# A chunked scan in a three-block network: six places for the decay matrices, both directions added ahead of one product

## What is computed

```python
def step(h, inp):
    qq, kk, vv, aa = inp
    cs = jnp.cumsum(aa, axis=1)
    seg = cs[:, :, None] - cs[:, None, :]
    decay = jnp.exp(jnp.where(mask[None, :, :, None, None], seg, -jnp.inf))
    qk = jnp.einsum('bjgn,blgn->bjlg', qq, kk)
    y_intra = jnp.einsum('bjlgh,blghp->bjghp', qk[..., None] * decay, vv)
    y_inter = jnp.einsum('bjgn,bghnp->bjghp', qq, h) * jnp.exp(cs)[..., None]
    ...
def bidir_scan(q, k, v_f, v_b, a_f, a_b):
    y_f = chunked_scan(q, k, v_f, a_f, True)
    ...
    return y_f + y_b
```

## Time and profile before

| | |
|---|---|
| runs | 1742.20, 1742.33, 1742.42 us |
| the profiled execution | 1742.6 us, its span 1740.9 us |
| TensorE (PE) | 98% busy |
| VectorE (DVE), ScalarE (ACT), GpSimd (POOL) | 67%, 45%, 12% busy |
| chain that ended last | PE 84%, DVE 10%, ACT 4% |
| the scan stage | 1054.26 to 1282.62 us, four groups of 55 to 58 us |

### The profile page before, as it was taken

How to read it: one execution, slowest core, us unless ns; L and a number is a source line. 1 busy time by engine, 2 the same in 40 slices (tenths; PEclk the granted TensorE clock), 3 DMA queues, 4 the chain that set the end, 5 groups by cost and what they waited for, 6 DMA issues and landing times.

```text
span 1740.9 us, 21624 instructions
## 1 busy us (share of the span) xinstructions
PE 1709.1 (98%) x8558; PEld 1369.1 (79%) x8558; DVE 1171.2 (67%) x1646; ACT 790.0 (45%) x1364; POOL 210.1 (12%) x240
## 2 busy tenths in 40 slices
PE   9999999999999999999999999999989999999998
PEld 6887878776688888888897887776678888888887
DVE  5575774866668887663368996767773788766334
ACT  5565652642245454442244544475552455444221
POOL 1421001442000111110000000221120011111000
PEclk9999999999999999999999999999999999999999
DMA  6211223343222222233313221101113132223332
GB/s 225 98 61 49 73 85 133 96 85 79 67 73 97 98 97 97 97 97 100 96 65 115 85 97 61 37 25 37 37 49 109 62 111 97 98 97 93 98 100 70
DMA packets 45813, 150.04 MB, mean 86 GB/s; under 512 B 5776, under 2 KB 8976, under 8 KB 45584
## 3 DMA queue, kind: packets, MB, share of 16 engines
q1 hardware_dynamic: 41728, 141.89, 24.8%
q0 software_dynamic: 1536, 2.10, 1.1%
q10 hardware_dynamic: 2448, 4.66, 0.8%
HBM read 144.44 MB, written 2.10 MB: 84 GB/s over the span
## 4 chain that ended last, share of the span: by engine, by line
PE 84%; DVE 10%; ACT 4%; issue 1%; DMA 0%; POOL 0%; ACTq 0%; DVEq 0%
PE bank L388 23%; PE bank L390 22%; PE bank L389 22%; PE bank L405 2%; PE bank L407 2%; PE bank L406 2%; DVE w_lo L350 1%; DVE cv L2239 1%; ACT em L2458 1%; PE bank L2346 1%; PE bank L2305 1%; PE bank L985 1%; DVE em L2601 1%; PE bank L998 1%; PE bank L1483 1%
## 5 line engine op out<-in xcount | busy, mean ns | idle before, releaser
L388 PE MATMUL bank<-a_hi,w_hi 128*128 128x512 f32 x1384 | 554.8, 401 | 2.9 <-DVE a_lo L540 2.1
L350 DVE TENSOR_TENSOR w_lo<-raw,w_hi 128x1024 fp32r<-128x1024 f32 (+1 forms) x257 | 327.7, 1281 | 338.1 <-ACT w_hi L343 337.4
L390 PE MATMUL bank<-a_hi,w_lo 128*128 128x512 f32 x1384 | 539.3, 390 | 0.0
L389 PE MATMUL bank<-a_lo,w_hi 128*128 128x512 f32 x1384 | 538.9, 389 | 0.0
L343 ACT ACTIVATE w_hi<-raw 128x1024 fp32r<-128x1024 f32 (+1 forms) x259 | 268.4, 1043 | 305.9 <-DMA raw<-in_w_down 141.4
L388 PEld LDWEIGHTS bank<-a_hi,w_hi 128*128 128x128 f32 x1384 | 259.9, 188 | 76.4 <-issue 19.3
L389 PEld LDWEIGHTS bank<-a_lo,w_hi 128*128 128x128 f32 x1384 | 260.0, 188 | 58.4 <-issue 6.7
L390 PEld LDWEIGHTS bank<-a_hi,w_lo 128*128 128x128 f32 x1384 | 259.8, 188 | 55.0
L1355 ACT ACTIVATE u<-bank,par 128x512 f32<-128x512 f32 x88 | 68.6, 780 | 177.5 <-DVE bank L814 177.5
L1398 POOL TENSOR_TENSOR gv<-u 128x512 f32<-128x512 f32 x44 | 57.4, 1305 | 555.1 <-DVE u L1374 555.1
L388 PE MATMUL bank<-g_hi,w_hi 128*128 128x512 f32 x308 | 119.8, 389 | 0.0
(11 more groups left out here) (403 smaller groups left out, 2526.7 us busy)
## 6 DMA issues: line engine op xcount, KB each, us to landing
raw<-in_w_up SPq DMA_DIRECT2D x88, 512.0 KB, 3.2
raw<-in_w_in SPq DMA_DIRECT2D x50, 512.0 KB, 3.2
raw<-in_w_out SPq DMA_DIRECT2D x32, 512.0 KB, 3.7
raw<-in_w_down SPq DMA_DIRECT2D x32, 512.0 KB, 3.5
raw<-in_w_xbc SPq DMA_DIRECT2D x24, 512.0 KB, 3.2
raw<-in_w_z SPq DMA_DIRECT2D x16, 512.0 KB, 3.2
raw<-in_w_down SPq DMA_DIRECT2D x16, 384.0 KB, 3.1
raw<-in_w_mem_kv SPq DMA_DIRECT2D x4, 512.0 KB, 3.2
```

The lines of the kernel that those rows point to most:

```text
L350: nc.vector.tensor_tensor(w_lo[:, q % RING, 0:w], raw[:, q % RING, 0:w], w_hi[:, q % RING, 0:w].bitcast(F32), ALU.subtract).then_inc(lo_do ...
L388: nc.tensor.matmul(out, wh, rhs_hi[:, k, :], start=k == first, stop=False)
L389: nc.tensor.matmul(out, wh, rhs_lo[:, k, :], start=False, stop=False)
L390: return nc.tensor.matmul(out, wl, rhs_hi[:, k, :], start=False, stop=stop)
```

## The change

Two more homes for the matrices are added, `em4` and `em5`, and step n uses home n % 6. The exponentials of steps 0 to 5 are begun in the sweep. The passes are made by pairs: the matrices of the forward and the backward direction of a head are added, one head's by VectorE (`join`), the other's by GpSimd (`join_pool`), then weighed once each, and `inside(g, i)` makes one pass for a pair. The carried products are issued as transposes. Tile z2 moves ahead of the first group, and with it each later tile by one; the last group has one tile of z left instead of two, and 18 steps of out3 ahead of its last pass instead of 14. ScalarE's gates stand behind step 3 in all groups.

In the loops over the groups the diff below shows only the new lines and some of those that stay; what they replace stands in the kernel above.

```diff
+    em_more = [at("em4", [P, S], ST + 80), at("em5", [P, S], 97)]
+    matrix_home = [em[:, n, :] for n in range(4)] + [more[:, :] for more in em_more]
+    HOMES = len(matrix_home)
...
-                                 start=c == 0, stop=False, skip_group_check=True)
-
-        def inside(g, m):
-            i, half = m // 2, m % 2
-            pe.wait_ge(mlu, STEPS * g + 2 * m + 2)
+                                 start=c == 0, stop=False, is_transpose=True, skip_group_check=True)
+
+        def inside(g, i):
+            pe.wait_ge(mlu, HPG * g + 2 * i + 2)
             for c in range(TT):
-                for n in (2 * m, 2 * m + 1):
-                    hh = step_of(n)[1]
+                for hh in range(2):
                     mm = nc.tensor.matmul(bank[2 + i % 2][hh * HD:(hh + 1) * HD, c * P:(c + 1) * P],
-                                          xtok[:, c, (2 * i + hh) * HD:(2 * i + hh + 1) * HD], em[:, n % 4, c * P:(c + 1) * P],
-                                          start=False, stop=half == 1 and c == TT - 1, skip_group_check=True)
+                                          xtok[:, c, (2 * i + hh) * HD:(2 * i + hh + 1) * HD],
+                                          matrix_home[(4 * i + 2 * hh) % HOMES][:, c * P:(c + 1) * P],
+                                          start=False, stop=c == TT - 1, skip_group_check=True)
             mm.then_inc(intra, 1)
...
+        def spreads(g, *steps):
+            for n in steps:
+                spread(g, n)
+
+        def out3_pair(k):
+            out3_step(pe, 0, k)
+            out3_step(pe, 1, k)
+
+        for t in range(3):
             for q in range(4):
                 part_z(t, q)
+            if t < 2:
+                turn_x(0, range(2 * t, 2 * t + 2))
         tile_gone(pe, "xbc", 23)
         pe.wait_ge(xsilu, 24)
         pe.wait_ge(sel_done, 3)
         begin(0)
         for g in range(SG):
+            last = g == SG - 1
+            part_z(4 * g + 3, 0)
             if g:
+                turn_x(g, range(2, TT))
+            part_z(4 * g + 3, 1)
             states(g, 0)
+            part_z(4 * g + 3, 2)
+            spreads(g, 0, 1)
             between(g, 0)
+            part_z(4 * g + 3, 3)
             states(g, 1)
+            if last:
+                spreads(g, 2, 3)
+                between(g, 1)
+                out3_pair(0)
+                states(g, 2)
+                out3_pair(1)
+            else:
+                part_z(4 * g + 4, 0)
+                spreads(g, 2, 3)
+                part_z(4 * g + 4, 1)
+                between(g, 1)
+                part_z(4 * g + 4, 2)
+                states(g, 2)
+                part_z(4 * g + 4, 3)
+            spreads(g, 4, 5, 6, 7)
             between(g, 2)
             if g:
                 norm_sum(g - 1)
+            for i in range(4):
+                first, second = (4 * g + 5 + i // 2, 2 * (i % 2)), (4 * g + 5 + i // 2, 2 * (i % 2) + 1)
+                if i == 0:
+                    if last:
+                        out3_pair(2)
+                    else:
+                        part_z(*first)
+                        part_z(*second)
+                    carried(g, i)
                 else:
+                    carried(g, i)
+                    if last:
+                        out3_pair(2 * i + 1)
+                    else:
+                        part_z(*first)
+                    if i < 3:
+                        spreads(g, 4 * i + 4, 4 * i + 5)
+                    if not last:
+                        part_z(*second)
+                    elif i < 3:
+                        out3_pair(2 * i + 2)
+                    else:
+                        pe.wait_ge(e_x, STEPS * SG - 1)
+                        out3_step(pe, 2, 0)
+                        out3_step(pe, 2, 1)
+                if i == 3 and not last:
+                    begin(g + 1)
+                    turn_x(g + 1, range(2))
+                inside(g, i)
+                if i in (1, 2):
+                    spreads(g, 4 * i + 6, 4 * i + 7)
...
-            if n >= 4:
-                act.wait_ge(intra, 8 * g + n // 2 - 1)
+            if n >= HOMES:
+                act.wait_ge(intra, 4 * g + (n - HOMES) // 4 + 1)
...
+            last = g == SG - 1
+            hi_to(act, z0 + 4 * g + 6)
             if g:
                 squares(g - 1, 2)
                 squares(g - 1, 3)
+            decays(g, 0)
+            decays(g, 1)
+            if last:
+                tile_ready(act, "z", 4 * SG - 1)
+                high(0)
+            decays(g, 2)
+            decays(g, 3)
+            if last:
+                high(1)
+            hi_to(act, z0 + 4 * g + 7)
+            gates(g)
+            decays(g, 4)
+            decays(g, 5)
+            if last:
+                high(2)
+                high(3)
+            if g:
+                group_roots_act(g - 1)
+            hi_to(act, z0 + 4 * g + 8)
+            if last:
+                high(4)
+            for n in range(HOMES, STEPS):
...
+            join_pool(pool, g, 0)
             for i in range(4):
                 k = 4 * g + i
+                if i < 3:
+                    join_pool(pool, g, i + 1)
                 pool.wait_ge(yev, k + 1)
                 pool.wait_ge(zs_done, k + 1)
                 nc.gpsimd.tensor_tensor(xbc[:, k, :], xbc[:, k, :], zt[:, i, :], ALU.mult).then_inc(gated, 1)
...
+    def join_pool(pool, g, i):
+        n = 4 * i
+        forward, backward = matrix_home[(n + 2) % HOMES], matrix_home[(n + 1) % HOMES]
+        pool.wait_ge(e_x, STEPS * g + n + 3)
+        nc.gpsimd.tensor_tensor(forward, forward, backward, ALU.add).then_inc(joined, 1)
...
+        def join(g, i):
+            n = 4 * i
+            forward, backward = matrix_home[n % HOMES], matrix_home[(n + 3) % HOMES]
+            dve.wait_ge(e_x, STEPS * g + n + 4)
+            link("dve", dve, nc.vector.tensor_tensor(forward, forward, backward, ALU.add))
+
+        def weigh(g, i, hh):
+            if hh:
+                dve.wait_ge(joined, 4 * g + i + 1)
+            if i == 0 and hh == 0:
                 dve.wait_ge(gl_done, g + 1)
-            nc.vector.tensor_tensor(em[:, n % 4, :], em[:, n % 4, :], gmat[:, :], ALU.mult).then_inc(mlu, 1)
+            home = matrix_home[(4 * i + 2 * hh) % HOMES]
+            nc.vector.tensor_tensor(home, home, gmat[:, :], ALU.mult).then_inc(mlu, 1)
+
+        def pair_ready(g, i):
+            join(g, i)
+            weigh(g, i, 0)
+            weigh(g, i, 1)
...
+        for t in range(3):
+            take_z(t)
         for g in range(SG):
+            last = g == SG - 1
+            tailed(g, 0)
+            if g == 0:
                 masks(0)
             tailed(g, 1)
+            lo_to(dve, z0 + 4 * g + 4)
             grow(g, 1)
             carry(g, 0)
+            take_z(4 * g + 3)
             fed(g, 1)
             tailed(g, 2)
+            lo_to(dve, z0 + 4 * g + 5)
+            if last:
+                low(0)
             grow(g, 2)
             carry(g, 1)
+            if last:
+                low(1)
             fed(g, 2)
             carry(g, 2)
+            pair_ready(g, 0)
+            if last:
+                low(2)
+            if g:
+                root_half(g - 1)
+                root_first(g - 1)
+                root_second(g - 1)
+                root_third(g - 1)
+            evac_y(g, 0)
+            pair_ready(g, 1)
+            lo_to(dve, z0 + 4 * g + 6)
+            if last:
+                low(3)
+                low(4)
+            if g:
+                normed_y(g - 1, 0)
+                normed_y(g - 1, 1)
+            if not last:
+                take_z(4 * g + 4)
+            evac_y(g, 1)
+            if last:
+                low(5)
+            pair_ready(g, 2)
+            lo_to(dve, z0 + 4 * g + 7)
+            if last:
+                low(6)
+            if g:
+                normed_y(g - 1, 2)
+                normed_y(g - 1, 3)
+            if not last:
+                take_z(4 * g + 5)
+            evac_y(g, 2)
+            if last:
+                low(7)
+                lo_to(dve, z0 + 4 * g + 8)
+            pair_ready(g, 3)
+            if not last:
+                take_z(4 * g + 6)
+                masks(g + 1)
```

More of the change, by code:

```diff
@@ L2384, in ssd_pe @@
                 norm_sum(g - 1)
-            if g + 1 < SG:
-                for q in range(4):
-                    part_z(4 * g + 4, q)
-            for m in range(8):
-                if m < 7:
-                    spread(g, 2 * m + 2)
-                    spread(g, 2 * m + 3)
-                else:
-                    if g + 1 < SG:
-                        begin(g + 1)
-                if m % 2 == 0:
-                    carried(g, m // 2)
-                if m % 2 and g + 1 < SG:
-                    part_z(4 * g + 5, m // 2)
-                inside(g, m)
-                if g == SG - 1:
-                    for k in ((), (0, 1, 2), (), (), (3,), (4,), (5, 6), (7,))[m]:
-                        out3_step(pe, 0, k)
```

(15 more changed lines are left out.)

112 lines of the change are left out of this document (19 added, 93 removed).

## The result

| | median | runs | profiled execution, its span |
|---|---|---|---|
| before | 1742.20 us | 1742.07 to 1742.42 (5) | 1742.6, 1740.9 |
| after | 1750.04 us | 1748.61 to 1750.61 (5) | 1748.6, 1746.9 |

The ratio is 1.0043, with a 95% interval of 1.0032 to 1.0054. The forecast was 1736.0, with 1723 to 1746.

The account below looks back on a forecast made before the run. TensorE was taken to set the end. Start +6.9, first group -3.4, two middle groups -5.1 each and last group +0.4 gave -6.3 us from 1742.33: 1736.0, range 1723 to 1746.

Parts of the forecast that it names:

- The start: Ahead of the first state product: tile z2 and a quarter of z3, five quarters more on TensorE, +6.9 us.
- the prices of the pieces: TensorE times read from the earlier trace: quarter of z 1.38, pass 1.02, two spreads 0.46, four transposes 0.54 us.
- the waits of 2.1 in the sweep: Spreads 4 to 7 in a row on two banks: TensorE idles 1.3 ahead of spread 6, 0.8 ahead of 7.
- 1.2 for the second pair: Middle group: matrices ready 6.2 us behind the pass before, TensorE's own work 5.0, so it waits 1.2.
- GpSimd's 0.97: Added to each pair's weighings on VectorE because GpSimd's product with the gates runs beside them: 0.97 us.
- the third pair: Middle group, called pair 2: two spreads delay the exponentials by 0.5; ready at 6.7 against 5.6, wait 1.1 us.
- the last group, "+0.4": Last pass starts 57.4 us behind the group's first state product, before 57.1; claimed as +0.4.
- the walk: Following the engines' queues for work and waits: 4.4 us of waits in each of three groups, 21 in the last.
- The balance that stands beside the walk: Last group: 5.5 + 6.6 us of TensorE work gone, about 12 of waits come, given beside +0.4.
- give nothing: Behind the last pass: GpSimd's chain of squares sets what follows, so two early out3 steps of tile 2 gain nothing.
- Rival B: Last group at 1.2 GHz from its first out3 product, pieces on the path doubled: +15 us, 1751; chance 0.10.

## Why the prediction was wrong

Counted on the profiled executions, where it should have come out at 1736.3 and came out at 1748.6 (12.3; the rows below add up to 12.5, the rest is rounding):

| | forecast | measured | miss |
|---|---|---|---|
| first state product | 1061.1 | 1060.89 | -0.2 |
| group 0 | 51.6 | 51.77 | +0.2 |
| group 1 | 52.5 | 52.65 | +0.1 |
| group 2 | 52.5 | 54.28 | +1.8 |
| last group to its last pass | 57.4 | 65.3 | +7.9 |
| last pass to end | 459.3, as before | 462.0 | +2.7 |

**Right.** The start (+6.9), the prices of the pieces, the waits of 2.1 in the sweep (2.1), of 1.2 for the second pair (1.29), and GpSimd's 0.97. For the third pair I had 1.1; it is 0.40 and 0.88 for zt, 1.3 together. VectorE had room for what it was given in groups 0 to 2.

**The step that failed is the last group, "+0.4".** I walked 21 us of waits into 57 us and then priced every piece between them as at full clock. The pieces were at 1.2 GHz behind the waits: 5.2 of the 7.9, by the added work. The other 2.7 are mostly the walk itself: 0.7 ahead of the first pass, where the clock was 0.66 behind the wait for low(0), mostly hidden by low(1), and 0.6, 0.4 and 1.0 between the passes, at a clock of 1.00 (a part of these may be the added work running past its wait). The balance that stands beside the walk is loose too: TensorE loses five quarters of z behind the first state product, not four (seven in the kernel before, two now), and gains four steps of out3 ahead of the last pass. The 57.4 came from the walk and doesn't rest on it.

**The same cause in two places that I left at nothing.** Group 2's 1.8: the sweep's waits, which I had placed rightly, were followed by the products of `between` at the lower clock. Groups 0 and 1 have the same waits and kept a clock of 1.00. Which group this hits differs between executions, and I can't say why: in the profile of the kernel with the earlier low halves group 0 had it too (53.5), and in that of the changed kernel with plain carried products no group before the last had it (group 2 was 53.5, as long as group 1). And around the norm sum:

```profile
1295.00:1300.00 5.00, 4.95 (x13) 3.44 (x14) 4.80 (x6) 2.81 (x4) 0.00 (x0) 0.66 0.00 0
...
1284.91 1.52 PE L2347 MATMUL bank<-em,xtok 128*64 128x128 f32 x16 [2.06 <-DVE em L2660]
...
1295.05 1.50 PE L2451 MATMUL bank<-xbc,cst 128*128 128x512 f32 x2 [3.14 <-POOL xbc L2593]
```

In the earlier trace rows the norm sum waits 1.00, here 3.14. Before, ten steps of out3 stood between the last pass and the norm sum, now six do: the last pair of tiles 0 and 1 and the two early steps of tile 2 had covered the wait and now stand ahead of the last pass. I wrote that the two "give nothing"; they took away a cover. The 462.0 are 10.1 up to the norm sum (before 9.1) and 451.9 behind it (before 450.2). The 1.7 are behind the wait, where the clock was 0.66. Of the 1.0, 0.4 is the last pass itself, which took 1.52 instead of 1.09 behind its wait of 2.06; with 64 added products that pass took 1.09 and the norm sum came 9.7 behind it. The other 0.6 fit GpSimd's chain of squares, beside VectorE's four low halves in a row:

```profile
1287.14 4.67 DVE L2704 TENSOR_TENSOR y_lo<-xbc,y_hi 128x512 fp32r<-128x512 f32 x4
...
1288.92 1.74 POOL L2593 TENSOR_TENSOR xbc<-xbc 128x512 f32<-128x512 f32 x1
```

(that addition took 1.29 in the kernel before; this was read, not tried).

**Rival B had the mechanism, at a chance of 0.10, but not the size.** TensorE ran at 0.50 in 1260 to 1265, behind its longest wait. The Trainium skill, TensorE: Matmul & The Clock Gate, section What's actually happening, says that the clock is gated to half by how busy the engine has been, and the trace agrees. The rival put 15 on the last group and said that more than 6 of it would make the kernel slower. The clock took 5.2 there, so that by the rival's own count it would not have sufficed. It also took 1.6 to 1.8 in group 2, 0.4 in the last pass and 1.7 behind the norm sum, about 9 in all; with the walk's 2.7 and GpSimd's 0.6 this is the 12.3. By the profiled executions, an estimate: without the clock the change would have given about 3 us. The rival had the earlier trace rows for it, 0.90 and 0.76 where TensorE waited far less, so that its chance should have been the largest, and its price should have been worked out for every wait of the walk, not for one stretch.

What stays open: why the median is 1.4 above the profiled execution. Its clock was 0.992, that of the three slower runs 0.990 and 0.991, which points to the same cause in another number of places, but these have no trace.

Of GpSimd beside VectorE I had taken 0.97 a pair, and the changed kernel shows 0.98. By the Trainium skill, SBUF — State Buffer, section Who interferes with whom, the ports that VectorE and GpSimd share are an exclusive lock, and the price would have been 1.27, an estimate. The weighings show less. So do two normed tiles of the experiment with the late evacuation, 1.03 longer beside one GpSimd product; 2.03 was the price beside a product and a join.

## What to carry over

When a change takes work from the engine that sets the end, walk the new waits first, and price what stands behind each of them at the clock that rows of the same kernel show behind waits. A long wait on TensorE can cost twice, as itself and in what runs behind it, and moving independent work into it can pay twice: here two reorderings of a few lines turned +7.8 into -16, and one more, with VectorE's joins in the first group, into -20. Look also at what an operation that is moved had covered where it stood.

## What was new about the chip

- Adding 64 products (14.7 us of work) to TensorE's waits made the kernel 5.9 us faster: the granted clock behind these waits was 1.00 instead of 0.50 to 0.87.
- Waits of 1.0 and 0.5 us close together, in a group with TensorE 92% busy, were followed by the lower clock in some groups and executions and not in others. Five runs of the changed kernel spread over 2.0 us, five of the kernel before over 0.35 (27 later ones over 1.5). Where this spread comes from is open: with the last group's waits filled it was 4.9 over 11 runs.
- Beside one GpSimd operation two VectorE operations took 1.0 longer (2.27 instead of 1.29, 2.43 instead of 1.40), beside two 2.0 longer (3.43), and moving GpSimd's work away from one operation moved the cost to the next.
